# Per-head norms of a three-block kernel rewritten with compact roots, the third block's mixer outputs kept in SBUF, and two passes in the seven-product routine

## The chip, the cores and the metric

One core of a Trainium2 chip runs the whole program in one launch. The metric is device time in microseconds (us); lower is better. All data are float32. TensorE is called PE here, VectorE DVE, ScalarE ACT, GpSimd POOL, and SyncE (whose queue issues most transfers) SP.

## The reference, cut to what matters

Activations are 1024 positions by 1024 channels and pass through three blocks. The change touches the norms over single heads of 64 channels in blocks two and three, the end of the mixers of block three, and the gated and ungated MLPs of blocks three and one:

```python
def head_rmsnorm(o, gain):                                   # block 2: two mixers, 4 heads each, then * silu(gate)
    o = o * lax.rsqrt(jnp.mean(o * o, axis=-1, keepdims=True) + NORM_EPS_2)
...
    mean = jnp.mean(y, axis=-1, keepdims=True)               # block 3, rwkv: 8 heads
    var = jnp.mean(jnp.square(y - mean), axis=-1, keepdims=True)
    y = ((y - mean) * lax.rsqrt(var + LNX_EPS)).reshape(B, T, RWKV_DIM) * lnx_w + lnx_b
    y = y + bonus.reshape(B, T, RWKV_DIM)
    return y * g
...
    q = heads(rmsnorm(q.reshape(B, T, FOX_HEADS, HEAD_DIM), q_norm_w).reshape(B, T, FOX_DIM))   # block 3, fox
    k = heads(rmsnorm(k.reshape(B, T, FOX_HEADS, HEAD_DIM), k_norm_w).reshape(B, T, FOX_DIM))
...
    o = rmsnorm(o, o_norm_w).reshape(B, T, FOX_DIM)
    return o * jax.nn.sigmoid(og)
...
        x = x + jnp.concatenate([y_rwkv, y_fox], axis=-1) @ w_out[l].astype(jnp.float32)
        h = rmsnorm(x, norm_ffn_w[l])
        x = x + conv_glu_ffn(...)
```

## The kernel before

Activations lie transposed: 128 channels (two heads) on the partitions, 1024 positions along the free axis; such a 128x1024 tile is 512 KB. The program is a sequence of stages. Each `Stage` allocates its SBUF, PSUM and semaphores; when one that has semaphores ends, all engines meet at a barrier (L40), so nothing of the next stage starts before the slowest queue of this one is done, its stores included. Inside a stage each engine runs its own list and waits on semaphores.

`head_norm` (four calls: `hgn` in block two, `fqk`, `lnx` and `fon` in block three) takes one tile at a time from a scratch tensor in HBM: SP loads x, a gate and, in `lnx`, a bonus into one of three slots (L681 to L685; a slot is loaded again when its store has landed); ACT squares it (L721); PE multiplies with a 128x128 matrix of ones over each head, so that every row of the result holds its head's sum (L691); DVE makes the variance (L749); ACT takes the logarithm and the exponential (L93, L94); DVE makes a Newton step of three operations (L99 to L101) and the product with gain and root (L759); POOL multiplies with the gates and issues the store (L784 to L792). In `lnx`, PE and DVE first subtract the mean (L744).

`rwkv_and_fox` (stage `mix`) runs the two mixers of block three interleaved from one job list. Its outputs leave for HBM from POOL (wkv in 16 pieces, fox in 4); `lnx` and `fon` read them back and store to `y3`. `folded_project` then computes `w_out` (stage `p`) with Strassen-like seven products for each pair of output tiles: before the first product it loads its eight input tiles (`feed`, L497), and DVE makes sums of input tiles (L244 to L250). The residual X stays in SBUF for the whole of blocks one to three (`stream_x`), and is added in `scaled_sum` (`res3a`).

`Folded.products` is that routine of seven products, each accumulated over kp pairs of input tiles. In `mlp`, hidden tiles are made in groups ("up" jobs) and each group is followed by four "down" jobs; the first of these four calls `products` with `await_last`, which waits (`u_sums`) for DVE's sums of the last pair of hidden tiles (L448). kp is 4 in block one's MLP; in block three's (`mlp3`) it is 3 in three groups and 2 in the last.

## Time and profile before

| what | value |
|---|---|
| median of 3 runs | 5811.05 us (5807.86 to 5812.35) |
| the profiled execution | 5812.52 us, its span 5810.9 us |
| PE busy | 4890.9 us, 84% |
| DVE, ACT, POOL busy | 2521.5, 1119.2, 898.6 us |
| mean granted PE clock | 0.921 of full |

The span runs from the first to the last instruction; the profiled execution lasted 1.6 us longer than its span. Busy time of PE is modelled from a pipelined engine, so PE busy is not PE at its peak.

### The profile page before, as it was taken

How to read it: one execution, taken by the hardware profiler on the slowest of the kernel's cores; microseconds unless marked ns; L12 is line 12 of the kernel's file. 1: busy time of each engine (PE TensorE's matmuls, PEld its weight loads, DVE VectorE, ACT ScalarE, POOL GpSimd, SP SyncE). 2: the span in 40 equal slices, each digit the busy share in tenths (PEclk: the TensorE clock that was granted, in tenths of full speed). 3: DMA queues.
4: the chain of work that ended last, by engine and by line, in shares of the span. 5: the costliest groups of instructions: out<-in, count | busy, mean ns of one | idle time of the engine just before them, and what ended most of it. 6: DMA issues, size and time to landing. Idle time of an engine off the chain costs nothing. (4 is left out here: it accounts for less than half of the span.)

```text
span 5810.9 us, 44089 instructions
## 1 busy us (share of the span) xinstructions
PE 4890.9 (84%) x16320; PEld 2512.2 (43%) x16320; DVE 2521.5 (43%) x3261; ACT 1119.2 (19%) x1602; POOL 898.6 (15%) x674
## 2 busy tenths in 40 slices
PE   8988677899997988889858597857999728999995
PEld 3434343344443434335523243326888613444442
DVE  4305552634554212225334414554443344755755
ACT  1003231100001003333220101243344321110101
POOL 0014401222221110012011010000000031222220
PEclk9999898999998999889979798978999869999997
DMA  2121202111111221111131013332221121111111
GB/s 99 58 102 34 76 37 91 69 44 44 44 44 62 87 86 39 37 65 63 61 138 43 33 73 115 141 111 65 53 53 48 50 103 66 38 42 43 40 44 69
DMA packets 194463, 378.61 MB, mean 65 GB/s; under 512 B 102919, under 2 KB 104471, under 8 KB 193368
## 3 DMA queue, kind: packets, MB, share of 16 engines
q1 hardware_dynamic: 173320, 315.10, 16.0%
q0 software_dynamic: 12880, 46.14, 2.2%
q10 hardware_dynamic: 8064, 14.68, 0.7%
q8 instruction: 128, 2.10, 0.1%
q14 instruction: 71, 0.58, 0.0%
HBM read 270.84 MB, written 105.02 MB: 65 GB/s over the span
## 5 line engine op out<-in xcount | busy, mean ns | idle before, releaser
L157 PE MATMUL mlp_bank<-mlp_u,mlp_s 128*128 128x512 f32 x864 | 380.9, 597 | 0.0
L889 PE MATMUL first_acc<-first_h,first_w 128*128 128x512 f32 x768 | 332.9, 594 | 0.0
L157 PE MATMUL mlp_bank<-mlp_u,mlp_w 128*128 128x512 f32 x648 | 293.1, 604 | 38.8 <-DVEq L448 38.8
L157 PE MATMUL p_bank<-p_t,p_s 128*128 128x512 f32 x720 | 313.9, 592 | 0.0
L144 POOL TENSOR_TENSOR mlp_s<-mlp_w 128x512 f32<-128x512 f32 (+2 forms) x70 | 90.2, 1288 | 1330.2 <-DMA mlp_w<-in_w_up 749.0
L157 PE MATMUL mlp_bank<-stream_x,mlp_s 128*128 128x512 f32 x608 | 273.3, 592 | 0.0
L157 PE MATMUL mlp_bank<-mlp_x,mlp_s 128*128 128x512 f32 x608 | 273.3, 592 | 0.0
L157 PE MATMUL mlp_bank<-stream_x,mlp_w 128*128 128x512 f32 x608 | 267.1, 592 | 0.0
L157 PEld LDWEIGHTS mlp_bank<-mlp_u,mlp_s 128*128 128x128 f32 x864 | 166.0, 192 | 210.8 <-issue 208.6
L2598 PE MATMUL rwin_half<-in_h,rwin_w 128*128 128x512 f32 x512 | 237.5, 624 | 10.8 <-ACT rwin_half_out L2647 10.8
L215 ACT ACTIVATE mlp_p<-mlp_bank 128x512 f32<-128x512 f32 x70 | 41.4, 591 | 989.6 <-PE mlp_bank L157 989.6
L889 PEld LDWEIGHTS first_acc<-first_h,first_w 128*128 128x128 f32 x768 | 144.9, 190 | 186.4 <-issue 186.4
L157 PEld LDWEIGHTS p_bank<-p_t,p_s 128*128 128x128 f32 x720 | 136.8, 190 | 172.2 <-issue 169.6
L157 PEld LDWEIGHTS mlp_bank<-mlp_u,mlp_w 128*128 128x128 f32 x648 | 124.8, 193 | 197.4 <-issue 155.3
L225 DVE TENSOR_TENSOR mlp_sum_u<-mlp_bank,mlp_p 128x512 f32<-128x512 f32 x70 | 48.4, 692 | 349.9 <-PE mlp_bank L157 348.5
L1622 PE MATMUL stick_tile<-stream_x,stick_fw 128*128 128x512 f32 x384 | 185.4, 628 | 0.0
L157 PEld LDWEIGHTS mlp_bank<-mlp_x,mlp_s 128*128 128x128 f32 x608 | 115.5, 190 | 145.4 <-issue 141.6
L157 PEld LDWEIGHTS mlp_bank<-stream_x,mlp_s 128*128 128x128 f32 x608 | 115.5, 190 | 145.4 <-issue 142.8
L157 PEld LDWEIGHTS mlp_bank<-stream_x,mlp_w 128*128 128x128 f32 x608 | 115.5, 190 | 145.4 <-issue 145.2
L2039 PE MATMUL lin_tile<-stream_x,lin_w 128*128 128x512 f32 x384 | 176.4, 608 | 0.0
L2598 PEld LDWEIGHTS rwin_half<-in_h,rwin_w 128*128 128x128 f32 x512 | 101.8, 200 | 147.8 <-issue 133.7
L144 POOL TENSOR_TENSOR p_s<-p_w 128x512 f32<-128x512 f32 x30 | 39.8, 1327 | 803.0 <-DMA p_w<-in_w_in 519.6
(621 smaller groups left out, 8460.8 us busy)
## 6 DMA issues: line engine op xcount, KB each, us to landing
mlp_w<-in_w_up SPq DMA_DIRECT2D x76, 512.0 KB, 4.1
proj<-p_ev SPq DMA_DIRECT2D x38, 512.0 KB, 2.7
p_w<-in_w_in SPq DMA_DIRECT2D x36, 512.0 KB, 5.7
mlp_w<-in_w_down SPq DMA_DIRECT2D x32, 512.0 KB, 4.6
first_w<-in_w_in SPq DMA_DIRECT2D x24, 512.0 KB, 3.2
p_w<-in_w_out SPq DMA_DIRECT2D x24, 512.0 KB, 5.7
merge_g<-proj SPq DMA_DIRECT2D x8, 1536.0 KB, 8.1
mlp_w<-in_w_down SPq DMA_DIRECT2D x24, 384.0 KB, 3.5
```

The lines of the kernel that those rows point to most:

```text
L144: nc.gpsimd.tensor_tensor(s1, a21, a22, ALU.add).then_inc(self.sums_ready, 1)
L157: mm = nc.tensor.matmul(self.bank[product - 1][:, :], lhs[:, p, :], rhs(name, p), start=p == 0, stop=p == kp - 1)
L215: nc.scalar.activation(self.p1[:, :], self.bank[0][:, :], ACT.Copy).then_inc(self.copied, 1)
L225: ch.step(nc.vector.tensor_tensor(self.u[:, :], p6, self.p1[:, :], ALU.add))
L889: mm = nc.tensor.matmul(acc[m % 2][:, cs], W[m % 2][:, k * P:(k + 1) * P], H[:, k, cs], start=k == 0, stop=k == KD - 1)
L1622: mm = nc.tensor.matmul(tile_acc[:, :], fw[t % 2][:, k * P:(k + 1) * P], act_in[:, k, e * HT:(e + 1) * HT], start=k == 0, stop=k == KD - 1)
L2039: mm = nc.tensor.matmul(tile_acc[h][:, :], W[t % 2][:, k * P:(k + 1) * P], act_in[:, k, h * HT:(h + 1) * HT], start=k == 0, stop=k == KD - 1)
L2598: mm = nc.tensor.matmul(half_acc[h][:, :], W[t % 2][:, k * P:(k + 1) * P], act_in[:, k, h * HT:(h + 1) * HT], start=k == 0, stop=k == KD - 1)
```

## The change

`head_norm` is replaced by `compact_norm`. It holds all tiles of a call in SBUF, in groups of four tiles (eight heads). PE sums the squares of a group with a 128x8 matrix (`pick`) into one 8x1024 result, one row for each head. Variance, logarithm, exponential and Newton step run once for each group on 8 partitions, after one load of an ACT table set. PE spreads each root over its 64 channels by a product with an 8x128 matrix (`back`), into a ring of two PSUM tiles that DVE reads as operand. POOL applies gates ahead of the root instead of behind it; stores are issued by SP. In the kind "layer" the bonus and beta are multiplied with the gate on DVE and added at the end. `lnx` and `fon` become one call, `lfn`, that reads the mixer outputs from a tensor Y in SBUF, and `p32` multiplies this Y directly. X gives up its place in SBUF during the mixers: `n21` stores it to HBM (`kept2`) and `p32` loads it back (`also`, L501 of the kernel before: issued by POOL behind the last sums). With `await_last`, `products` now makes all seven products over the first kp-1 pairs, waits, and then adds the last pair to all seven.

```diff
+        def all_seven(pairs, fresh, done):
+            if fresh:
...
+            await_product("B11")
+            mm = some(1, a11, "B11", pairs)
+            if done:
+                mm.then_inc(self.phases_done, 1)
...
+        if await_last is None:
+            all_seven(range(kp), True, True)
+            all_seven(range(kp - 1), True, False)
             await_last()
...
+            all_seven([kp - 1], False, True)
...
-def head_norm(nc, name, src, dsts, heads_ones, width, gain, eps, scale=1.0, gate=None, gate_kind=None,
...
+def compact_norm(nc, name, X, groups, width, heads, pick_in, back_in):
...
+        var, root, fix = ([r.sb(f"{n}{gi}", [8, T]) for gi in range(NG)] for n in ("var", "root", "fix"))
...
+        total = [r.ps(f"total{gi}", [8, T]) for gi in range(NG)]
+        ring = [r.ps(f"ring{s}", [P, T]) for s in range(2)]
...
+                sp.dma_start(pick[:, :], pick_in).then_inc(picks_in, 16)
+                sp.dma_start(back[:, :], back_in).then_inc(picks_in, 16)
...
+                            sp.dma_start(x_of(gi, j), g["src"][j]).then_inc(x_in[gi, j], 16)
...
+                            sp.dma_start(G[gi, j][:, :], g["gate"][j]).then_inc(g_in[gi, j], 16)
...
+                            sp.dma_start(A[gi, j][:, :], g["add"][j]).then_inc(a_in[gi, j], 16)
...
+                        if g.get("dst") is not None:
+                            sp.wait_ge(finished, n)
+                            for a, b, d in g["dst"](j):
+                                sp.dma_start(d, x_of(gi, j)[a:b, :]).then_inc(sent, 16)
...
+                def sums(n):
+                    gi, j = sq_order[n]
+                    pe.wait_ge(sq_ready, n + 1)
+                    for cs in (LEFT, RIGHT):
+                        mm = nc.tensor.matmul(total[gi][:, cs], pick[:, 8 * j:8 * j + 8], sq[n % 4][:, cs],
+                                              start=j == 0, stop=j == len(groups[gi]["tiles"]) - 1)
+                    mm.then_inc(sq_used, 1)
...
+                for gi, j in mean_order:
...
+                        pe.wait_ge(ring_free, no - 1)
+                    both(ring[no % 2], heads[:, :], x_of(gi, j)).then_inc(ring_done, 1)
+                pe.wait_ge(picks_in, 32)
+                for n in range(len(sq_order)):
+                    sums(n)
+                for gi, g in enumerate(groups):
+                    pe.wait_ge(rstd_ready, gi + 1)
+                    for j in range(len(g["tiles"])):
+                        no = ring_no["back", gi, j]
...
+                            pe.wait_ge(ring_free, no - 1)
+                        both(ring[no % 2], back[:, j * P:(j + 1) * P], root[gi]).then_inc(ring_done, 1)
...
+                def roots(gi):
+                    act.wait_ge(var_ready, gi + 1)
+                    inverse_root(nc, ach, root[gi], var[gi][:, :], exp_ready)
+                for n, (gi, j) in enumerate(sq_order):
...
+                    if groups[gi]["kind"] == "layer":
+                        act.wait_ge(centred, mean_order.index((gi, j)) + 1)
+                    if n >= 4:
+                        act.wait_ge(sq_used, n - 3)
+                    nc.scalar.activation(sq[n % 4][:, :], x_of(gi, j), ACT.Square).then_inc(sq_ready, 1)
+                    if n == ends[gi] and groups[gi]["kind"] in ("sigmoid", "silu"):
+                        for i in range(len(groups[gi]["tiles"])):
+                            act.wait_ge(g_in[gi, i], 16)
+                            nc.scalar.activation(SG[gi, i][:, :], G[gi, i][:, :], ACT.Sigmoid).then_inc(sig_ready, 1)
+                nc.scalar.preload_act_table_set("natural_log_exp_and_others")
+                for gi in range(NG):
+                    roots(gi)
+            @block.gpsimd
+            def _(pool):
...
+                for key in pool_order:
...
+                    x, kind = x_of(gi, j), groups[gi]["kind"]
+                    pool.wait_ge(sq_ready, sq_no[key] + 1)
+                    pool.wait_ge(g_in[key], 16)
...
+                    if kind in ("silu", "layer"):
+                        ch.step(nc.gpsimd.tensor_tensor(x, x, G[key][:, :], ALU.mult))
+                    if kind != "layer":
+                        pool.wait_ge(sig_ready, gate_order.index(key) + 1)
+                        ch.step(nc.gpsimd.tensor_tensor(x, x, SG[key][:, :], ALU.mult))
+                    pool.sem_inc(gated, 1)
...
+                for gi, j in mean_order:
+                    dve.wait_ge(ring_done, ring_no["mean", gi, j] + 1)
...
+                    nc.vector.scalar_tensor_tensor(x_of(gi, j), ring[ring_no["mean", gi, j] % 2][:, :], -1.0 / width,
+                                                   x_of(gi, j), ALU.mult, ALU.add).then_inc(centred, 1)
+                    dve.wait_ge(centred, mean_order.index((gi, j)) + 1)
+                    dve.sem_inc(ring_free, 1)
+                def variance(gi):
+                    dve.wait_ge(sq_used, ends[gi] + 1)
+                    nc.vector.tensor_scalar(var[gi][:, :], total[gi][:, :], 1.0 / width, groups[gi]["eps"], ALU.mult, ALU.add)\
+                      .then_inc(var_ready, 1)
+                variance(0)
...
+                for gi, g in enumerate(groups):
+                    dve.wait_ge(exp_ready, gi + 1)
+                    newton(nc, ch, root[gi][:, :], var[gi][:, :], fix[gi][:, :])
+                    dve.sem_inc(rstd_ready, 1)
+                    if gi + 1 < NG:
+                        variance(gi + 1)
+                    if g["kind"] == "layer":
+                        for j in range(len(g["tiles"])):
...
+                            ch.step(nc.vector.scalar_tensor_tensor(A[gi, j][:, :], A[gi, j][:, :], g["beta"][j], G[gi, j][:, :],
+                                                                   ALU.add, ALU.mult))
+                    for j in range(len(g["tiles"])):
+                        no, x = ring_no["back", gi, j], x_of(gi, j)
+                        dve.wait_ge(ring_done, no + 1)
...
+                        if g["kind"] != "plain":
+                            dve.wait_ge(gated, pool_no[gi, j] + 1)
+                        ch.step(nc.vector.scalar_tensor_tensor(x, x, scaled_gain[:, n:n + 1], ring[no % 2][:, :],
+                                                               ALU.mult, ALU.mult))
+                        dve.sem_inc(ring_free, 1)
+                        if g["kind"] == "layer":
+                            ch.step(nc.vector.tensor_tensor(x, x, A[gi, j][:, :], ALU.add))
+                        dve.sem_inc(finished, 1)
...
-def scaled_sum(nc, name, x, alpha, y, store=None):
+def scaled_sum(nc, name, x, alpha, y, dst=None, store=None):
...
-                        nc.scalar.activation(YO[c % 2][:, :, :], of(job)[:, :, 0:CK], ACT.Copy).then_inc(kept["y"], 1)
+                        nc.scalar.activation(Y[:, 0:NP, c * CK:(c + 1) * CK], of(job)[:, :, 0:CK], ACT.Copy).then_inc(kept["y"], 1)
...
-                        nc.vector.tensor_copy(Y[h // 2 % 2][e, i * P:w], O[e, 0:P]).then_inc(o_kept, 1)
+                        nc.vector.tensor_copy(Y[e, NP + h // 2, i * P:w], O[e, 0:P]).then_inc(o_kept, 1)
...
-                        pool.dma_start(wkv_out[c], YO[c % 2][:, :, :]).then_inc(y_sent[c % 2], 16)
-                        pool.dma_start(fox_out[j], Y[j % 2][:, :]).then_inc(fox_sent[j % 2], 16)
...
+    heads = np.arange(P)[:, None, None] // 64 + 2 * np.arange(4)[None, :, None] == np.arange(8)[None, None, :]
...
+    c["back"] = heads.transpose(2, 1, 0).reshape(8, 4 * P)
...
-            head_norm(nc, "hgn", lambda j: heads2[j * P:(j + 1) * P, :],
...
+            with Stage(nc, "hgnx") as q:
+                hx = q.sb("x", [P, 4, T])
+                compact_norm(nc, "hgn", [hx[:, j, :] for j in range(4)],
+                             [{"kind": "silu", "tiles": range(4), "src": [heads2[j * P:(j + 1) * P, :] for j in range(4)],
...
-                normalise(nc, "n21", M, X, ones, col["ln_g"], EPS2, beta=col["ln_b"])
+                normalise(nc, "n21", M, X, ones, col["ln_g"], EPS2, beta=col["ln_b"], store=tile_rows(kept2))
...
-            head_norm(nc, "fqk", lambda j: proj3[f0 + j * P:f0 + (j + 1) * P, :],
...
+            with Stage(nc, "fqkx") as q:
+                hx = q.sb("x", [P, 8, T])
...
+                def split_heads(to):
+                    return lambda j: [(h * HD, (h + 1) * HD, to[2 * j + h, 0:HD, :]) for h in range(2)]
+                compact_norm(nc, "fqk", [hx[:, j, :] for j in range(8)],
+                             [{"kind": "plain", "tiles": range(4 * i, 4 * i + 4), "scale": (HD ** -0.5, 1.0)[i], "eps": EPS,
+                               "src": [proj3[f0 + j * P:f0 + (j + 1) * P, :] for j in range(4 * i, 4 * i + 4)],
+                               "gain": columns(col[("fq", "fk")[i]]), "dst": split_heads((qa, ka)[i])} for i in range(2)],
...
-            head_norm(nc, "lnx", lambda j: wkv[j * P:(j + 1) * P, :], lambda j: [(0, P, y3[j * P:(j + 1) * P, :])],
...
-            head_norm(nc, "fon", lambda j: fox[j * P:(j + 1) * P, :], lambda j: [(0, P, y3[512 + j * P:512 + (j + 1) * P, :])],
...
+        with Stage(nc, "tail") as tail:
+            Y = tail.sb("y", [P, KD, T])
+            rwkv_and_fox(nc, rw, qa, ka, proj3[f0 + 1024:f0 + 1536, :], c["chunk_mask"], c["chunk_wide"], c["causal"], ident, Y)
+            compact_norm(nc, "lfn", [Y[:, j, :] for j in range(8)],
+                         [{"kind": "sigmoid", "tiles": range(4, 8), "eps": EPS, "gain": columns(col["fo"]),
+                           "gate": [proj3[f0 + 1536 + j * P:f0 + 1536 + (j + 1) * P, :] for j in range(4)]},
+                          {"kind": "layer", "tiles": range(4), "eps": 64e-5, "gain": columns(col["lnx_w"]),
+                           "beta": columns(col["lnx_b"]), "add": [rw["bonus"][j * P:(j + 1) * P, :] for j in range(4)],
+                           "gate": [rw["gate"][j * P:(j + 1) * P, :] for j in range(4)]}], HD, heads64, c["pick"], c["back"])
             with Stage(nc, "out3") as q:
-                Y, M = q.sb("y", [P, KD, T]), q.sb("m", [P, KD, T])
-                folded_project(nc, "p32", Y, a["w_out3"], KD, dst=M, feed=[tile_rows(y3)[n] for n in range(KD)])
-                scaled_sum(nc, "res3a", M, 1.0, X, store=tile_rows(kept3))
+                M, X = q.sb("m", [P, KD, T]), q.sb("x", [P, KD, T])
+                folded_project(nc, "p32", Y, a["w_out3"], KD, dst=M, also=(X[:, :, :], rows(kept2)))
+                scaled_sum(nc, "res3a", M, 1.0, X, dst=Y, store=tile_rows(kept3))
+            X = Y
```

## Rows read from the trace of the kernel before

**Rows 1.** Windows: hgn, fqk, mix, lnx, fon, p32's matmuls, res2 with n21.
```profile
core 0: us, PE busy (x) PEld busy (x) DVE busy (x) ACT busy (x) POOL busy (x), PEclk, DMA share, GB/s
2886.50:2952.60 66.10, 12.80 (x16) 4.44 (x16) 28.96 (x24) 32.19 (x28) 21.98 (x12) 0.55 0.25 95
3836.70:3924.60 87.90, 25.17 (x32) 8.33 (x32) 49.12 (x48) 45.66 (x40) 8.48 (x16) 0.62 0.33 96
3940.70:4604.30 663.60, 608.16 (x4832) 557.75 (x4832) 266.68 (x573) 256.84 (x521) 13.74 (x19) 0.97 0.20 48
...
4610.60:4694.70 84.10, 20.18 (x32) 7.67 (x32) 39.94 (x32) 22.83 (x20) 23.70 (x12) 0.60 0.25 100
4694.70:4755.40 60.70, 12.85 (x16) 4.38 (x16) 25.22 (x24) 32.19 (x28) 11.71 (x8) 0.58 0.28 104
...
4772.00:4871.30 99.30, 98.59 (x224) 43.30 (x224) 30.38 (x44) 2.39 (x4) 9.94 (x8) 0.98 0.07 23
...
3189.00:3261.50 72.50, 32.74 (x64) 13.69 (x64) 39.69 (x37) 13.13 (x12) 0.00 (x0) 0.74 0.00 0
```

**Rows 2.** Groups by tile and line: duration ns min/median/max, first and last start.
```profile
L99 DVE TENSOR_TENSOR fqk_fix<-fqk_rstd x8: 1212/1216/1224, 3849.6 to 3912.4; 128x1024 f32<-128x1024 f32 x8
...
L749 DVE TENSOR_SCALAR fqk_var<-fqk_total x8: 1215/1224/1225, 3844.9 to 3906.3; 128x1024 f32<-128x1024 f32 x8
...
L759 DVE SCALAR_TENSOR_TENSOR fqk_x<-fqk_x,fqk_gain,fqk_rstd x8: 1284/1284/1285, 3853.4 to 3916.2; 128x1024 f32<-128x1024 f32 x8
...
L786 POOL TENSOR_TENSOR hgn_x<-hgn_x,hgn_g x4: 2328/2336/2343, 2907.4 to 2943.1; 128x1024 f32<-128x1024 f32 x4
...
L2165 ACT ACT_TABLE_LOAD  x1: 1283/1283/1283, 2591.1 to 2591.1; - x1
```

**Rows 3.** Timeline of ACT in fqk: the first two squares.
```profile
3839.90 1.06 ACT L721 ACTIVATE fqk_sq<-fqk_x 128x1024 f32<-128x1024 f32 x1 [6.44 <-DMA fqk_x<-proj]
3841.17 1.06 ACT L721 ACTIVATE fqk_sq<-fqk_x 128x1024 f32<-128x1024 f32 x1 [0.22 <-DMA fqk_x<-proj]
```

**Rows 4.** DVE in lnx beside a busy POOL; DVE operation with a PSUM operand.
```profile
4679.73 3.25 DVE L101 SCALAR_TENSOR_TENSOR lnx_rstd<-lnx_fix,lnx_rstd 128x1024 f32<-128x1024 f32 x1
...
4678.69 3.20 POOL L786 TENSOR_TENSOR lnx_x<-lnx_x,lnx_g 128x1024 f32<-128x1024 f32 x1
...
L225 DVE TENSOR_TENSOR mlp_sum_u<-mlp_bank,mlp_p x70: 690/692/693, 1077.1 to 5743.7; 128x512 f32<-128x512 f32 x70
```

**Rows 5.** Timeline of PE in lnx: two tiles, then one tile.
```profile
4616.92 6.86 PE L691 MATMUL lnx_mean<-lnx_x,main_heads 128*128 128x512 f32 x8 [12.94 <-DMA lnx_a<-rw_bonus]
4623.62 1.88 PE L691 MATMUL lnx_total<-lnx_sq,main_heads 128*128 128x512 f32 x4
```

**Rows 6.** Timeline around res3a: a bare barrier, and one behind stores.
```profile
4872.34 9.17 DVE L2440 SCALAR_TENSOR_TENSOR stream_x<-out_m,stream_x 128x1024 f32<-128x1024 f32 x8 [1.00 <-PEq L40]
...
4886.09 2.00 ACT L364 ACTIVATE mlp3m_m<-stream_x 128x1024 f32<-128x1024 f32 x2 [35.44 <-PEq L40]
```

**Rows 7.** Timeline of p32's start.
```profile
4755.40 43.95 SPq L133 DMA_DIRECT2D p_w<-in_w_out  x6
...
4773.25 3.21 DVE L244 TENSOR_TENSOR p_t<-out_y 128x512 f32<-128x512 f32 x4 [25.01 <-DMA out_y<-y]
...
4760.44 1.26 POOL L144 TENSOR_TENSOR p_s<-p_w 128x512 f32<-128x512 f32 x1 [0.41 <-DMA p_w<-in_w_out]
...
4772.02 9.32 PE L157 MATMUL p_bank<-out_y,p_w 128*128 128x512 f32 x16 [39.63 <-DMA out_y<-y]
```

**Rows 8.** PE's waits in mlp3: their sum, the first, the last.
```profile
  PE mlp_bank L157: 38.8, 4
...
5063.92 3.78 PE L157 MATMUL mlp_bank<-mlp_u,mlp_w 128*128 128x512 f32 x4 [9.02 <-DVEq L448]
5067.49 8.30 PE L157 MATMUL mlp_bank<-mlp_u,mlp_s 128*128 128x512 f32 x16
...
5699.40 3.78 PE L157 MATMUL mlp_bank<-mlp_u,mlp_w 128*128 128x512 f32 x4 [11.77 <-DVEq L448]
```

More of the change, by code:

```diff
@@ L166, in await_bank @@
                 pe.wait_ge(self.banks_free, 4 * (n - 1) + count)
-        now, late = range(kp), []
-        if await_last is not None:
-            now, late = range(kp - 1), [kp - 1]
-        self.await_weights(pe, n)
-        if n:
-            pe.wait_ge(self.copied, n)
-        await_product("B11")
-        mm = some(1, a11, "B11", now)
-        if not late:
-            mm.then_inc(self.phases_done, 1)
-        await_bank(1)
-        await_product("B21")
-        mm = some(2, a12, "B21", now)
@@ L571, in normalise @@
             if store is not None:
-                assert add_to is not None
+                assert add_to is not None or beta is not None
                 @block.sync
@@ L675, in _ @@
             def _(sp):
-                for j in range(N):
-                    s = j % 3
-                    if j >= 3:
-                        sp.wait_ge(stored[s], 16 * len(dsts(0)) * (j // 3))
-                    sp.dma_start(X[s][:, :], src(j)).then_inc(loaded[s], 16)
-                    if gate is not None or times is not None:
-                        sp.dma_start(G[s][:, :], (gate or times)(j)).then_inc(loaded[s], 16)
-                    if add is not None:
-                        sp.dma_start(A[s][:, :], add(j)).then_inc(loaded[s], 16)
+                sp.dma_start(pick[:, :], pick_in).then_inc(picks_in, 16)
@@ L687, in _, with both @@
             @block.tensor
             def _(pe):
[L689 to L708 removed]
+                def both(out, lhs, x):
+                    for cs in (LEFT, RIGHT):
+                        mm = nc.tensor.matmul(out[:, cs], lhs, x[:, cs], start=True, stop=True)
+                    return mm
@@ L737, in _ @@
                 ch = Chain(dve, own)
-                for j in range(N):
-                    ins = nc.vector.tensor_scalar(scaled_gain[:, j:j + 1], gain[j], scales[j], None, ALU.mult)
-                ch.step(ins)
-                def take_mean(j):
-                    dve.wait_ge(mean_ready, j + 1)
-                    nc.vector.scalar_tensor_tensor(X[j % 3][:, :], mean[j % 2][:, :], -1.0 / width, X[j % 3][:, :],
-                                                   ALU.mult, ALU.add).then_inc(centred, 1)
@@ L2448, in _ @@
                         sp.wait_ge(own, k + 1)
-                        sp.dma_start(store[k], y[:, k, :]).then_inc(stored, 16)
+                        sp.dma_start(store[k], dst[:, k, :]).then_inc(stored, 16)
                     sp.wait_ge(stored, 16 * KD)
@@ L2805, in mix_jobs, with rwkv_and_fox @@
     return jobs
[L2808 removed]
+def rwkv_and_fox(nc, src, q, k, v, masks_in, wide_in, causal_in, ident, Y):
     NP = RH // 2
@@ L2842, in rwkv_and_fox @@
         PT = r.sb("pt", [P, KD, P])
-        Y = [r.sb(f"y{s}", [P, T]) for s in range(2)]
         st = r.sb("st", [P, 2, 4])
@@ L3489, in build @@
-            head_norm(nc, "lnx", lambda j: wkv[j * P:(j + 1) * P, :], lambda j: [(0, P, y3[j * P:(j + 1) * P, :])],
-                      heads64, HD, columns(col["lnx_w"]), 64e-5, centre=True, beta=columns(col["lnx_b"]),
-                      add=lambda j: rw["bonus"][j * P:(j + 1) * P, :], times=lambda j: rw["gate"][j * P:(j + 1) * P, :])
-            head_norm(nc, "fon", lambda j: fox[j * P:(j + 1) * P, :], lambda j: [(0, P, y3[512 + j * P:512 + (j + 1) * P, :])],
-                      heads64, HD, columns(col["fo"]), EPS, gate=lambda j: proj3[f0 + 1536 + j * P:f0 + 1536 + (j + 1) * P, :],
-                      gate_kind="sigmoid")
+            with Stage(nc, "fqkx") as q:
[6 more added lines that the diff above has]
+                               "gain": columns(col[("fq", "fk")[i]]), "dst": split_heads((qa, ka)[i])} for i in range(2)],
+                             HD, heads64, c["pick"], c["back"])
```

261 lines of the change are left out of this document (108 added, 153 removed).

## The prediction

> **What bounds the kernel now.** I read the busy times first: PE is busy 84% of the span, but that is a mean over stages, so the windows by stage come next [rows 1]: each row gives the length of a stage and how long each engine was busy in it. In mix and in p32 PE works nearly all the time (608.2 of 663.6 us, 98.6 of 99.3). In the four calls of the head norm no engine does: in fqk PE is busy 25.2 of 87.9 us, DVE 49.1, ACT 45.7, and the DMA engines a third. These stages are chains: load, square, sum, root, Newton, product, store, with three slots between the loads and the stores. Together hgn, fqk, lnx and fon take 66.1 + 87.9 + 84.1 + 60.7 = 298.8 us. Since every stage ends in a barrier, a microsecond won in a norm is a microsecond of the end, and only what is won inside a stage behind PE counts nothing. The last views are the start of p32, where PE waits for input tiles that were just stored [rows 7], and PE's waits in mlp3 [rows 8].
>
> **Prices.** A 512 KB load lands 3.2 us after its issue and then one each 1.27 us [rows 3]; the stage and its first issue began at 3836.7 [rows 1]. ACT takes 1.06 for 1024 columns [rows 3], a table load 1.28 [rows 2]. DVE takes 1.22 for an operation of 1024 columns and 1.28 for the product with gain and root; POOL 2.34 [rows 2]. The change works on 8 partitions instead of 128 in variance, root and Newton step. No row prices that shape; an operation can hardly be dearer than on 128, and it walks the same 1024 columns, so I take 1.06 and 1.22, with nothing as the lower bound. PE needs 3.44 us for a tile of two halves at 1.2 GHz (8 records in 6.86 us) and 1.72 at 2.4 GHz [rows 5], the two levels of its clock; PE had idled 12.9 us before the stretch at the lower one. The products with `pick` and `back` stream the same 512 columns, so I price them as L691. A bare barrier costs 1.0; from DVE's last operation (4872.34 + 9.17 = 4881.5) behind a store to the next stage's first work it is 4.6 [rows 6].
>
> When DVE and POOL both work on SBUF, one DVE operation took 3.25 instead of 1.22 and one of POOL 3.20 instead of 2.34; with an operand in PSUM DVE's time stayed at 0.69 in all 70 cases [rows 4]. The Trainium skill (SBUF — State Buffer, section "SBUF: two separate sides") says that a DVE operation with two SBUF inputs and a GpSimd operation exclude each other and the loser blocks for the whole operation. That speaks against this change, which puts the gates of POOL beside the Newton step; by that rule alone a Newton operation could wait 2.3 us, about what the row shows, and the trace agrees.
>
> **hgn.** Times from the stage's start. Two small constants are issued first (0.8), then x and gate in turn: x lands at 4.0, 6.6, 9.1, 11.7. The last square ends at 12.7, PE's sums at 15.6, the variance at 16.8. ACT goes on after the squares: table 1.3, four sigmoids 4.3, table 1.3, root 2.1, so 21.8. That is later than the variance; ACT sets this step. The Newton step costs 3.7 alone. POOL has eight products, seven of them behind the first sigmoid (15.1): 7 x 2.4 = 17, so until 32 to 35, beside the Newton step, which may therefore take up to 3 x 3.25 = 9.8. The root is ready between 25.6 and 31.6; I take 29. PE has been idle since 15.6, so two of four tiles run at the lower clock: 10.3. DVE's last product is at 40.9, the store and barrier add 4.6: 46, against 66.1. Gain 20 (42 to 51, so 15 to 24).
>
> **n21.** The store of X to `kept2` is new. Its first seven tiles hide behind DVE's remaining products; the last adds 4.6 - 1.0. Loss 3.7 (3 to 5), on a stage chain of 72.5 us [rows 1].
>
> **fqk.** Eight tiles land from 4.0 to 12.9. PE's sums, in order and two of them at the lower clock, set the step: first group at 15.5, second at 22.3. Group one: variance 16.8, ACT free of its squares and its table load at 17.9, root 20.1, Newton 23.9. PE then spreads four tiles (until 31) and DVE multiplies behind it until 32.4. DVE does the Newton step of group two only then: 36.2. PE has idled for 5; four tiles take 7 at the upper clock or 10.3 with two at the lower: last product at 46, plus 4.6: 51, against 87.9. There is no POOL work in it. Gain 37 (33 to 40).
>
> **mix, lnx, fon.** DVE's last copy in mix ends at 4604.3, p32 starts at 4755.4: 151.1 us for the drain of the last stores, lnx and fon. In their place: barrier 1.0, lfn, barrier 1.0, no store at all. In lfn no input is awaited: Y is there. PE makes the four means (to 11), the sums of eight tiles follow to 24.5; ACT squares and makes the sigmoids beside it. Root of the fox group at 22, Newton beside POOL's last gates until 28 (26 free of POOL), variance of group two, PE's four tiles and DVE's products until 38. Then Newton 3.7, four times bonus plus beta times gate 5.0, four times product and sum 10.2: 57. PE's tiles of this group run under the 5.0 and cost nothing; without that cover, with PE at the lower clock, they would add 3. The twelve loads (12 x 1.27 + 4 = 19 us) land before DVE wants them. lfn 57 (52 to 64), in all 59 against 151.1. Gain 92 (85 to 97). Inside mix 20 stores go and their waits with them; they were covered by PE's 608 busy us, so I count nothing (a loss of 1 to a gain of 2).
>
> **p32.** It started PE at 4772.0, 16.6 us into the stage, though POOL had weights at 5.0. With Y in SBUF PE starts at 5.0. What is late next are DVE's sums of input tiles, 3.2 us for each of four kinds; they start at 0.3 and the first is done at 3.5, under PE's first two products of 9.3 us [rows 7]. Gain 11.7 (10 to 13). The load of X (eight times 1.27, about 10 us) is issued behind POOL's last sums, when PE is about half through its 99 us; it is hidden. Nobody queues behind it.
>
> **mlp3.** PE waits 38.8 us in four places for DVE's last sums: three times 9.0 and once 11.8 [rows 8]. The end of the wait is DVE's and stays. Moved ahead of it are three products over kp-1 pairs, of 0.86 us each: 3 x 2 x 0.86 = 5.15 in three groups, 3 x 0.86 = 2.6 in the last: 18.0. After the first wait 20 records took 11.9 us, where the upper clock takes 8.6 + 0.15; with a shorter idle some of this 3 us comes back: 3 in all (0 to 9). Against it: all seven results now finish within 6.0 us, and the next job waits for banks that DVE frees. DVE's four quarters are about 9 us of work in an accumulating job, but the next job needs them over its own first 5 us; I count up to 3. Gain 21 (16 to 27). mlp1 has no such wait to take from, and its PE never stops there: 0 (a loss of up to 2).
>
> **Sum.** 20 - 3.7 + 37 + 92 + 11.7 + 21 = 178.0 us. The profiled execution took 5812.5 us, 1.7 outside its span; the median of the runs is 5811.05, 1.5 lower. The change touches nothing outside the span: 5811 - 178 = 5633 us. All low ends give 151, all high ends 200.
>
> **Rivals.** (1) The chains stay long: POOL and DVE block each other through both gated norms and PE stays at 1.2 GHz in every product with `back`. For it: the norms ran at 0.55 to 0.62 of the clock [rows 1] and the 3.25 us row; against it: fqk has no POOL work, and lfn's PE hides. It costs 5 in hgn, 4 in fqk, 9 in lfn and 10 in mlp3's banks and p32 together, with 10 more for waits I don't see: 5640 to 5675, say 5665. The Trainium skill's rule (SBUF — State Buffer, section "SBUF: two separate sides") leads to this case, since a blocked DVE operation and a blocked GpSimd operation then hold each other up for as long as both have work. (2) More comes back than I count, because 8 partitions are cheaper, the clock stays up, or mix runs quicker without its stores; at 3% of mix's 663.6 us that is 20: 5600. (3) The seven-product change does not do what it says: PE waits for a bank where it waited for a sum. Its 21 us are lost: 5654. Against it: DVE frees the banks of the job before while PE makes 6.9 us of early products. (4) Slower: the outputs of mix written straight into Y hold up mix. There are 16 copies by ACT and 64 by DVE on its chain; the gain of 178 is gone when each costs 178 / 80 = 2.2 us more, that is when mix takes 27% longer. At 3 us each it is 5873. Against it: the same engines make the same number of copies of the same size, only the address differs.
>
> **Chances and range.** Forecast 0.74, rival 1 0.10, rival 2 0.07, rival 3 0.07, rival 4 0.02. The range 5604 to 5666 takes in all low and high ends and rival 3, and leaves out the far parts of 1 and 2. Two tenths of a per cent, 12 us, is what a measurement of this kernel can tell from no change: faster 0.97, within 0.01, slower 0.02.
>
> **What the profile would show.** lfn between 52 and 64 us long with no store; hgn about 46, fqk about 51; one table load before the roots of each call; PE's first product in p32 5 us after its first weight issue; PE's four waits in mlp3 at 3.9, 3.9, 3.9 and 9.2. The prediction is wrong if Newton steps on 8 partitions take much less or more than 3.7, if PE's products with 8 rows or 8 columns cost other than 0.43 a record, if a new wait stands in front of PE in mlp3, or if mix is not 663 us.

## The result and the profile after

The changed kernel took 5645.93 us (median of 4 runs, 5641.68 to 5659.12) against 5811.6 us for the kernel before on the same chip: a ratio of 0.972, with an interval of 0.9703 to 0.9737. The forecast was 5633 us with a range of 5604 to 5666; the gain is 165.7 us where 178 were forecast. The profiled execution took 5648.0 us, its span 5646.3.

First the windows by stage, as in [rows 1]: hgn, fqk, mix, lfn (which has the place of lnx and fon), p32.

```profile
core 0: us, PE busy (x) PEld busy (x) DVE busy (x) ACT busy (x) POOL busy (x), PEclk, DMA share, GB/s
2890.00:2940.09 50.09, 22.86 (x32) 6.52 (x32) 15.44 (x12) 12.80 (x12) 20.96 (x8) 0.60 0.32 127
...
3819.52:3879.70 60.18, 40.96 (x64) 12.30 (x64) 20.52 (x24) 13.95 (x13) 0.00 (x0) 0.65 0.46 140
3894.47:4554.77 660.30, 606.02 (x4832) 555.54 (x4832) 266.80 (x573) 255.63 (x520) 0.00 (x0) 0.98 0.18 43
4555.90:4619.39 63.49, 48.98 (x80) 15.77 (x80) 40.21 (x36) 18.81 (x18) 20.88 (x8) 0.71 0.26 100
4620.29:4726.30 106.01, 99.24 (x224) 43.56 (x224) 35.57 (x43) 2.39 (x4) 24.19 (x17) 0.94 0.21 80
```

The stages add up to the difference of the spans, 164.6 us:

| stretch | before, us | after, us | gain | forecast |
|---|---|---|---|---|
| start to hgn | 2886.5 | 2890.0 | -3.5 | 0 |
| hgn | 66.1 | 50.1 | 16.0 | 20 |
| hgn's end to fqk (with n21) | 884.1 | 879.4 | 4.6 | -3.7 |
| fqk | 87.9 | 60.2 | 27.7 | 37 |
| forget | 16.1 | 14.8 | 1.4 | 0 |
| mix | 663.6 | 660.3 | 3.3 | 0 |
| end of mix to p32 | 151.1 | 65.5 | 85.6 | 92 |
| p32 to the end | 1055.5 | 1026.0 | 29.5 | 32.7 |

Where the gain of a norm comes from shows in ACT's groups of fqk, before and after (busy time, mean of one, then the idle time ahead):

```profile
L93 ACT ACT_TABLE_LOAD x8 | 10.3, 1283 | 0.1
L94 ACT ACT_TABLE_LOAD x8 | 10.3, 1283 | 0.1
L721 ACT ACTIVATE fqk_sq<-fqk_x 128x1024 f32<-128x1024 f32 x8 | 8.4, 1052 | 29.8 <-DMA fqk_x<-proj 29.8
...
L771 ACT ACT_TABLE_LOAD x1 | 1.3, 1283 | 0.0
L766 ACT ACTIVATE fqk_sq<-fqkx_x 128x1024 f32<-128x1024 f32 x8 | 8.4, 1056 | 10.2 <-DMA fqkx_x<-proj 10.2
```

Sixteen table loads became one and sixteen root operations four, but ACT's waits for x also fell from 29.8 to 10.2 us, since no load waits for a slot any more. No run takes the fewer roots and the missing slots apart.

What fell short is hgn, fqk and lfn by 19.7 us together, and the last stretch by 3.2. In hgn, DVE's timeline shows the Newton step, PE's the product with `back`, and DVE's again the products behind it.

```profile
2912.10 2.28 DVE L99 TENSOR_TENSOR hgn_fix<-hgn_root 8x1024 f32<-8x1024 f32 x1 [5.43 <-ACT hgn_root L94]
2914.41 3.24 DVE L100 SCALAR_TENSOR_TENSOR hgn_fix<-hgn_fix,hgn_var 8x1024 f32<-8x1024 f32 x1
2917.69 3.24 DVE L101 SCALAR_TENSOR_TENSOR hgn_root<-hgn_fix,hgn_root 8x1024 f32<-8x1024 f32 x1
...
2921.05 14.02 PE L723 MATMUL hgn_ring<-hgn_root,hgn_back 8*128 8x512 f32 x16 [15.71 <-DVEq L818]
...
2928.28 1.28 DVE L834 SCALAR_TENSOR_TENSOR hgnx_x<-hgnx_x,hgn_gain,hgn_ring 128x1024 f32<-128x1024 f32 x1 [2.13 <-PE hgn_ring L723]
```

The Newton step takes 8.8 us; I had allowed up to 9.8 and counted a part of it. The four tiles of the spread take 14.02 us, which is 16 records at 1.2 GHz, to the last one: I had written 10.3. Behind the first tile DVE waits 2.13 us for PE in each. The granted clock of this stretch is 0.50; in lfn the sums with `pick` ran at 1.00:

```profile
core 0: us, PE busy (x) PEld busy (x) DVE busy (x) ACT busy (x) POOL busy (x), PEclk, DMA share, GB/s
2921.05:2935.07 14.02, 14.02 (x16) 5.14 (x16) 3.84 (x3) 0.00 (x0) 4.43 (x2) 0.50 0.27 107
4562.98:4576.88 13.90, 13.90 (x33) 2.80 (x32) 4.62 (x4) 9.66 (x10) 12.30 (x6) 1.00 0.79 316
```

The spreads in fqk are the more telling, since to the first of them PE comes from products at 2.4 GHz (its timeline):

```profile
3834.73 5.31 PE L730 MATMUL fqk_total<-fqk_sq,fqk_pick 128*8 128x512 f32 x12
3842.23 11.62 PE L723 MATMUL fqk_ring<-fqk_root,fqk_back 8*128 8x512 f32 x16 [2.19 <-DVEq L818]
3859.25 14.02 PE L723 MATMUL fqk_ring<-fqk_root,fqk_back 8*128 8x512 f32 x16 [5.40 <-DVEq L818]
```

At 0.43 us a record at the upper clock and 0.876 at the lower (14.02 / 16), 11.62 us are about five records at the upper clock and eleven at the lower: PE was busy all the time and its clock fell.

In mlp3 PE's waits went as forecast, three of 3.88 us and one of 9.16 (their sum in the view of the waits, then the first in PE's timeline), against [rows 8].

```profile
PE mlp_bank L157 <- DVEq L454: 20.8, 4, 9.2
```

```profile
4920.17 3.52 PE L157 MATMUL mlp_bank<-mlp_u,mlp_w 128*128 128x512 f32 x4 [3.88 <-DVEq L454]
4923.53 3.60 PE L157 MATMUL mlp_bank<-mlp_u,mlp_s 128*128 128x512 f32 x8
```

### The profile page after: what moved, and what is told of

Its sections match the earlier page's. It is cut to its first block and busy times, and to the rows that moved or that the text cites. A ratio compares the mean times of both kernels' runs of the same rounds, so it can differ in the third digit from the quotient of the medians.

```text
span 5646.3 us, 44066 instructions
## 1 busy us (share of the span) xinstructions
PE 4932.6 (87%) x16400; PEld 2520.4 (45%) x16400; DVE 2466.3 (44%) x3205; ACT 1026.9 (18%) x1525; POOL 862.3 (15%) x615
## 5 line engine op out<-in xcount | busy, mean ns | idle before, releaser
L157 PE MATMUL mlp_bank<-mlp_u,mlp_w 128*128 128x512 f32 x648 | 293.3, 603 | 20.8 <-DVEq L454 20.8
L157 PE MATMUL mlp_bank<-tail_y,mlp_s 128*128 128x512 f32 x352 | 158.2, 592 | 0.0
L157 PE MATMUL mlp_bank<-tail_y,mlp_w 128*128 128x512 f32 x352 | 154.7, 592 | 0.0
L221 ACT ACTIVATE p_p<-p_bank 128x512 f32<-128x512 f32 x30 | 17.9, 597 | 748.6 <-PE p_bank L157 748.6
L157 PE MATMUL mlp_bank<-mlp_x,mlp_w 128*128 128x512 f32 x304 | 136.7, 592 | 0.0
```

Source lines behind the costliest of these rows:

```text
L157: mm = nc.tensor.matmul(self.bank[product - 1][:, :], lhs[:, p, :], rhs(name, p), start=p == 0, stop=p == kp - 1)
L221: nc.scalar.activation(self.p1[:, :], self.bank[0][:, :], ACT.Copy).then_inc(self.copied, 1)
```

## The experiments

Nine edited kernels and the changed kernel once more. Lengths in us from the first DMA issue of a stage to that of the next; lfn has its barriers with it, and fqk is taken to the third issue of forget, so it is 0.7 longer here than above.

| run | time | ratio | hgn | to fqk | fqk | to lfn | lfn | p32 to the end |
|---|---|---|---|---|---|---|---|---|
| changed | 5645.9 | 0.9720 | 50.1 | 879.4 | 60.9 | 675.5 | 64.4 | 1026.0 |
| changed, again | 5645.9 | 0.9717 | 49.7 | 873.5 | 63.3 | 678.7 | 64.4 | 1026.7 |
| old products | 5668.2 | 0.9761 | 50.9 | 879.0 | 61.2 | 677.2 | 64.4 | 1043.8 |
| 128 rows | 5626.6 | 0.9689 | 46.0 | 876.8 | 52.5 | 675.7 | 59.1 | 1025.5 |
| PE kept busy | 5636.3 | 0.9704 | 47.5 | 877.3 | 60.3 | 675.6 | 62.2 | 1024.7 |
| gate on DVE | 5641.5 | 0.9719 | 45.1 | 878.1 | 63.2 | 678.1 | 62.3 | 1026.3 |
| combined | 5627.4 | 0.9685 | 43.9 | 882.1 | 50.7 | 677.8 | 60.1 | 1024.9 |
| round trip | 5693.9 | 0.9801 | 50.0 | 872.6 | 63.5 | 678.6 | 12.9 + 86.2 | 1036.7 |
| 32 rows | 5648.1, one run | | 50.1 | 876.3 | 61.0 | 677.5 | 64.1 | 1027.0 |
| 64 rows | 5641.5, one run | | 50.1 | 879.9 | 55.6 | 675.8 | 64.1 | 1027.1 |
| balanced | 5621.6 | 0.9673 | 43.5 | 871.1 | 50.3 | 677.7 | 58.0 | 1026.6 |

The intervals of the ratios are 0.0013 to 0.0017 to either side. The stretch from hgn to fqk is the same code in all eleven and runs from 871.1 to 882.1; hgn began anywhere from 2886.6 to 2893.8. So these two rows of the table of gains (-3.5 and 4.6) can't be read to the microsecond. Where its code is the changed kernel's, hgn repeats within 1.2 (49.7 to 50.9), fqk within 2.6 (60.9 to 63.5, the gate on DVE among them, which alters nothing in fqk) and lfn within 0.1.

**The control.** 

> The changed kernel itself, as the measure for the runs beside it. Stage lengths should repeat within 1 us (hgn 50, fqk 60, lfn 64), the beginning of hgn anywhere between 2886 and 2894 as in the runs so far, and the time 5640 to 5650 us.

 Time, hgn and lfn are as expected; fqk is 2.4 us longer than in the first profile, so it repeats less well than I wrote: its sums took 16.69 us where they had taken 15.32, and the first spread 13.03 where it had taken 11.62.

**The old products.**

```diff
-            all_seven(range(kp - 1), True, False)
             await_last()
-            all_seven([kp - 1], False, True)
+            some(1, a11, "B11", late).then_inc(self.phases_done, 1)
+            some(2, a12, "B21", late).then_inc(self.phases_done, 1)
+            some(5, s1, "T1", late).then_inc(self.phases_done, 1)
+            some(7, s3, "T3", late).then_inc(self.phases_done, 1)
...
+        some(6, s2, "T2", range(kp)).then_inc(self.phases_done, 1)
```

> The changed kernel with the products of mlp3 in the old order (T1, T3 and the last pair before T2, B22 and T4). Theory (the wait of PE shrinks by the moved products, 18.0 us, and some 3 us of clock come back): PE waits 38.8 us again in mlp3, three times 9.0 and once 11.8, the stage is 18 to 21 us longer and the kernel takes 5664 to 5667 us. Rival (the moved products cost as much in waits for banks in the next job): under 5 us, 5646 to 5651. A side question: in the changed kernel hgn begins 3.5 us later than before; if the new order does that in mlp1, hgn begins near 2886.5 here, otherwise near 2890.

 5668.2 us, 22.3 more and 1.2 above my range; the profiled spans differ by 20.6. The view of waits has 38.8 us again. The last stretch is 17.8 us longer, but it holds two stages that moved apart: p32 with res3a is 2.0 shorter here (119.6 against 121.6, its weights land earlier), and mlp3, from ACT's first operation in it to the end, is 19.9 longer (924.3 against 904.4; the kernel before has 924.8). The waits account for 18.0. In the other nine profiles with the new order mlp3 takes 904.2 once and 906.0 to 906.8 eight times, so of the 3 us of clock that I added some 2 were there in two profiles of ten and none in the rest. The rival of the banks falls. hgn began at 2890.3, but with the new order it began anywhere from 2886.6 to 2893.8, so this one value settles nothing about the side question.

```profile
PE mlp_bank L157 <- DVEq L448: 38.8, 4, 11.7
```

**128 rows.**

```diff
-        pick, back, picks_in = r.sb("pick", [P, 32]), r.sb("back", [8, 4 * P]), r.sem("picks_in")
+        pick, back, picks_in = r.sb("pick", [P, 32]), r.sb("back", [P, 4 * P]), r.sem("picks_in")
...
+                for gi in range(NG):
+                    nc.gpsimd.memset(root[gi][:, :], 0.0).then_inc(zeroed, 1)
```

Here root is [P, T], and `back` is filled up with zero rows and loaded behind the inputs. 

> The root tile and the matrix `back` have 128 rows, 120 of them zero, so the product that spreads the root is 128x128 by 128x512 as in the kernel before. Theory (a product of 8 rows leaves PE at 1.2 GHz, one of 128 rows lets it rise): four tiles take 10.4 to 10.6 us instead of 14.0 where PE had idled, and about 7 in the first group of fqk instead of 11.6; hgn 3.4 us shorter, fqk 3 to 8, lfn 3 to 5, in all 10 to 15: 5631 to 5636 us. Rival A (the clock is low only because PE had idled, and four tiles are too short for it to rise): 14.0 us stay, 5646. Rival B (zero rows do no work, so 120 more of them change nothing): 14.0 and 11.6 stay, 5646.

 5626.55 us, 19.4 less, more than I expected; 17.8 of it lies in the three norms. PE's timeline, the spreads of hgn and of fqk:

```profile
2922.26 9.70 PE L724 MATMUL hgn_ring<-hgn_root,hgn_back 128*128 128x512 f32 x16 [15.79 <-DVEq L823]
...
3836.35 7.11 PE L724 MATMUL fqk_ring<-fqk_root,fqk_back 128*128 128x512 f32 x16 [2.28 <-DVEq L823]
3848.85 8.93 PE L724 MATMUL fqk_ring<-fqk_root,fqk_back 128*128 128x512 f32 x16 [5.39 <-DVEq L823]
```

The idle time ahead (15.79, 2.28, 5.39) is as in the changed kernel; and 14.02, 11.62 and 14.02 become 9.70, 7.11 and 8.93. The edit also loads `back` later and clears the roots on POOL, but so do the runs with 32 and 64 rows below, where a spread from idle stays at 14 us; what is left is the rows. Both rivals fall: the 120 added rows hold zeros, and the clock rises with them. Two windows inside the spread of hgn show it:

```profile
2922.26:2926.00 3.74, 3.74 (x5) 1.67 (x6) 0.00 (x0) 0.00 (x0) 3.66 (x2) 0.50 0.02 4
2927.00:2931.96 4.96, 4.96 (x11) 1.65 (x9) 2.89 (x3) 0.00 (x0) 0.00 (x0) 0.95 0.49 198
```

**PE kept busy.**

```diff
+                for _ in range({"hgn": 8, "fqk": 1, "lfn": 3}[name]):
+                    both(ring[0], heads[:, :], sq[(len(sq_order) - 1) % 4])
                 for gi, g in enumerate(groups):
                     pe.wait_ge(rstd_ready, gi + 1)
```

> PE makes unused products of 128 rows while it waits for the first root: 8 tiles' worth in hgn, 1 in fqk, 3 in lfn, so that it comes to the products with `back` at 2.4 GHz. Theory (the 8-row product itself pulls the clock down, as in the first group of fqk, where PE came to it 2.2 us after products at the upper clock and 16 records took 11.6 us): a first group takes 11 to 12 us instead of 14.0, so hgn and lfn are 2 to 3 us shorter each, fqk the same: 5640 to 5642 us. Rival (the idle time ahead is what sets the clock): a first group takes 7 us, hgn, fqk and lfn are 7, 4 and 6 us shorter: 5629 us. The second groups of fqk and lfn stay at 14.0 by both.

 hgn and lfn are 2.6 and 2.2 us shorter, as by the theory, and fqk 0.6, less than it moves by itself. The profiled span is 5.0 lower (5641.3 against 5646.3), as the stages have it; the median is 9.7 lower and below my range. The profiled execution was the slowest of its four (5643.0 against 5634.7 to 5637.8), and what the other 4 are isn't shown. PE's timeline in hgn, and two windows inside the spread:

```profile
2909.55 14.00 PE L723 MATMUL hgn_ring<-hgn_sq,main_heads 128*128 128x512 f32 x32
2925.34 10.90 PE L723 MATMUL hgn_ring<-hgn_root,hgn_back 8*128 8x512 f32 x16 [1.80 <-DVEq L822]
```

```profile
2925.34:2927.50 2.16, 2.16 (x5) 1.03 (x6) 0.14 (x1) 0.00 (x0) 2.09 (x1) 1.00 0.00 0
2928.00:2936.20 8.20, 8.20 (x11) 2.76 (x9) 3.20 (x3) 0.00 (x0) 1.86 (x1) 0.53 0.45 181
```

PE came in at 1.00 and was at 0.53 in the second window, with no idle time between. In fqk PE had no idle time ahead of the first spread either, only products of 128 rows at 1.00. The clock fell all the same:

```profile
3840.53 1.98 PE L723 MATMUL fqk_ring<-fqk_sq,main_heads 128*128 128x512 f32 x4
3842.45 9.84 PE L723 MATMUL fqk_ring<-fqk_root,fqk_back 8*128 8x512 f32 x16
...
3842.45:3846.00 3.55, 3.55 (x10) 1.54 (x10) 2.28 (x2) 2.11 (x2) 0.00 (x0) 1.00 0.00 0
3847.50:3852.20 4.70, 4.70 (x6) 1.33 (x4) 1.28 (x1) 0.00 (x0) 0.00 (x0) 0.50 0.83 236
```

A PE that comes in at the upper clock is not kept there by this product.

**32 and 64 rows.** The edit is that with 128 rows, with another number. 

> As the run with 128 rows, but root and `back` have 32 rows. If what pulls the clock down scales with the rows, 32 of them should be nearer to 8 than to 128: four tiles take 13 to 14 us from idle, and the first group of fqk falls to the lower clock later or not at all. If any width over 8 will do, they take 9 to 10 us, as 128 rows do.

 

> Root and `back` with 64 rows, between the 32 at which nothing changed and the 128 at which four tiles took 7.1 to 9.7 us. If the clock goes by the share of rows, something between: a group from idle in 10 to 13.5 us, and the first group of fqk falls late. If it has an edge between 32 and 128, a group takes either 14.0 or 9 to 10.

 PE's timeline with 32 rows, hgn then fqk, and with 64 rows in fqk:

```profile
2921.52 13.99 PE L724 MATMUL hgn_ring<-hgn_root,hgn_back 32*128 32x512 f32 x16 [15.78 <-DVEq L823]
...
3839.53 11.77 PE L724 MATMUL fqk_ring<-fqk_root,fqk_back 32*128 32x512 f32 x16 [2.43 <-DVEq L823]
```

```profile
3839.19 7.10 PE L724 MATMUL fqk_ring<-fqk_root,fqk_back 64*128 64x512 f32 x16 [1.78 <-DVEq L823]
3851.69 14.02 PE L724 MATMUL fqk_ring<-fqk_root,fqk_back 64*128 64x512 f32 x16 [5.39 <-DVEq L823]
```

32 rows are as 8. With 64 rows PE stayed at the upper clock in the one group to which it came at it (7.10) and never rose in the four to which it came from idle (14.02 here, 13.99 in hgn, 13.99 and 14.02 in lfn). My second guess had the 14.0 but not the 7.10, the first neither. Both kernels ran once; their times are not compared, only the groups.

**The gate on DVE.**

```diff
-                    if kind != "layer":
-                        pool.wait_ge(sig_ready, gate_order.index(key) + 1)
-                        ch.step(nc.gpsimd.tensor_tensor(x, x, SG[key][:, :], ALU.mult))
+                        if (gi, j) in SG:
+                            dve.wait_ge(sig_ready, gate_order.index((gi, j)) + 1)
+                            ch.step(nc.vector.tensor_tensor(x, x, SG[gi, j][:, :], ALU.mult))
```

> POOL keeps the products x by gate; the products by the sigmoid (four in hgn, four in lfn) are made by DVE just ahead of its product with gain and root, where it waits 2.1 us for PE in each tile. Theory (DVE and POOL block each other on SBUF): the Newton step of hgn takes 3.7 us instead of 8.8, that of lfn 3.7 to 6 instead of 8.4, and the moved products hide under PE: hgn 5 us shorter, lfn 2 to 5, kernel 5636 to 5639 us. Rival A (the Newton step is slow because of its 8 partitions or because DVE starts late on a root that ACT just wrote): 8.8 and 8.4 stay and the kernel takes 5646. Rival B (the moved products don't hide, DVE becomes the bound of the tiles): 8 x 1.25 = 10 us more, which takes back what the Newton step gives: 5646 to 5649.

 hgn is 5.0 us shorter and lfn 2.1, as expected; the median is only 4.4 lower, above my range. In its profile fqk, which the edit doesn't touch, is 2.3 longer and mlp3 2.1 (906.5 against 904.4), both within what they move by. Both rivals fall in hgn: the Newton step is quick, and the moved products hide. DVE's timeline in hgn:

```profile
2909.02 1.21 DVE L99 TENSOR_TENSOR hgn_fix<-hgn_root 8x1024 f32<-8x1024 f32 x1 [5.43 <-ACT hgn_root L94]
2910.26 1.21 DVE L100 SCALAR_TENSOR_TENSOR hgn_fix<-hgn_fix,hgn_var 8x1024 f32<-8x1024 f32 x1
2911.51 1.21 DVE L101 SCALAR_TENSOR_TENSOR hgn_root<-hgn_fix,hgn_root 8x1024 f32<-8x1024 f32 x1
```

The same three operations took 2.28, 3.24 and 3.24 us beside POOL. On 8 partitions they cost what they cost on 128 [rows 2], 1.21 us. The Trainium skill (SBUF — State Buffer, section "SBUF: two separate sides") says that a DVE operation with two SBUF inputs and a GpSimd operation that reads SBUF shut each other out; the trace agrees, with 2.0 us more for a DVE operation. In lfn POOL's four products x by gate are still beside the Newton step, and one operation of it took 3.25.

**The round trip put back.** A stage of its own stores the eight tiles of Y to `y3` behind mix; lfn gets `src` and `dst` in `y3`:

```diff
+                           "src": [tile_rows(y3)[j] for j in range(4, 8)], "dst": lambda j: [(0, P, tile_rows(y3)[4 + j])],
...
-                folded_project(nc, "p32", Y, a["w_out3"], KD, dst=M, also=(X[:, :, :], rows(kept2)))
+                folded_project(nc, "p32", Y, a["w_out3"], KD, dst=M, feed=[tile_rows(y3)[n] for n in range(KD)],
+                        also=(X[:, :, :], rows(kept2)))
```

> The changed kernel with the round trip put back: an own stage stores Y to `y3` behind mix, lfn loads its eight tiles from there and stores them again, and p32 feeds from `y3`. Theory (of the 86 us gained between mix and p32 some 35 are the round trip, the rest the new design): the storing stage takes 12 to 15 us, of which the kernel before hid all but about 5 in mix; lfn takes 85 to 92 us instead of 64, since PE waits for the last of 20 loads (4 + 17 x 1.27 = 25.6 us) before it squares; PE starts in p32 some 10 us later: 5690 to 5700 us. Rival (loads hide in lfn as they do in hgn and fqk, and nearly all of the gain is design): lfn at most 70, 5670 to 5680.

 5693.9 us, 48.0 more. The storing stage takes 12.9, lfn 86.2 instead of 64.4, and PE starts in p32 at 4671.40, 16.6 us into the stage, as it did before [rows 7], instead of 4.9 to 6.8. PE's timeline:

```profile
4584.35 6.63 PE L723 MATMUL lfn_ring<-tail_y,main_heads 128*128 128x512 f32 x8 [30.06 <-DMA tail_y<-y]
...
4671.40 8.98 PE L157 MATMUL p_bank<-tail_y,p_w 128*128 128x512 f32 x16 [23.21 <-DMA tail_y<-y]
```

The three lengths and the total are as the theory had them, but its "some 35" for the round trip was too much: 27.0. The gain of 85.6 us between mix and p32 splits so: 21.8 (86.2 - 64.4) are loads and stores of the norm; 5.2 are the wait for mix's last stores (6.3 us from DVE's last copy to lnx before, 1.1 to lfn after); the remaining 58.6 are what is left for the design: one call instead of two, one root for eight heads, no slots. No run splits them.

**Combined, then balanced.** Three edits in one (128 rows, the sigmoid's products on DVE, and the second Newton step ahead of the third product of group one):

```diff
                         dve.sem_inc(finished, 1)
+                        if j == 1 and gi + 1 < NG:
+                            step(gi + 1)
```

> Three edits together: `back` and root with 128 rows, the products by the sigmoid on DVE, and DVE's Newton step of the second group ahead of the third product of the first group instead of behind the fourth (in fqk and lfn), so that PE goes from group to group without the 5.4 us of idle time. Theory (what is left of the norms is a chain PE to DVE at the lower clock plus the DVE queue): hgn 50.1 to 41 us, fqk 60.2 to 46 (8.4 by the rows, 6 by the order), lfn 64.4 to 51 to 54, in all 33 to 36 us, 5610 to 5613 us. Rival (the three gains overlap, because DVE becomes the bound of each tile once PE is at 2.4 GHz: 1.23 + 1.28 + waits = 3.1 us where there is a gate): the order of the Newton step is worth nothing in lfn and the gate 2 us less in each: 20 to 24 us, 5622 to 5626.

 5627.4 us: no better than 128 rows alone. The rival's account holds, though its 5622 to 5626 was still too low. With PE at 2.4 GHz a tile with a gate costs DVE 2.96 us (from one product with gain and root to the next), and PE stands idle; hgn gains 2.1 us more, fqk 1.8, lfn loses 1.0. In fqk the early Newton step leaves PE 3.61 us idle, because both slots of the ring are full while DVE is at the root.

The last kernel leaves lfn's sigmoid products on POOL and moves the four operations bonus plus beta times gate (L825) into DVE's idle time:

```diff
+                prepare(mean_order[0:1])
                 variance(0)
+                prepare(mean_order[1:2])
...
+                step(0)
+                prepare(mean_order[2:])
```

> `back` and root with 128 rows; the sigmoid's products on DVE in hgn only; the second Newton step ahead of the third product of the first group; in lfn the four operations bonus plus beta times gate where DVE waits (one ahead of the first variance, one behind it, two behind the second). Theory (with PE at 2.4 GHz DVE's queue is the bound of lfn, so what counts is how much of it lies in DVE's idle time): hgn 44, fqk 51, lfn 53 us against 44, 51 and 60 in the combined run, so 20 us below the changed kernel in all, 5620 to 5624 us. Rival (the operations moved ahead block POOL's gates on SBUF and the gates become late instead): lfn 57 to 60, 5625 to 5629 us.

 5621.6 us, a ratio of 0.9673 (0.966 to 0.9686), the lowest median of all; the interval of the run with 128 rows (0.9672 to 0.9705) overlaps it. But lfn is 58.0, as by the rival, and not 53: POOL's gates took 2.73 to 3.84 us beside the moved operations and ended at 4567.8, 32.1 into the stage (29.4 in the changed kernel), so that two of the three Newton operations still took 3.25. POOL's timeline, the last two of its products by the sigmoid:

```profile
4547.69 2.73 POOL L793 TENSOR_TENSOR tail_y<-tail_y,lfn_sg 128x1024 f32<-128x1024 f32 x1 [0.57 <-ACT lfn_sq L768]
4550.69 3.84 POOL L793 TENSOR_TENSOR tail_y<-tail_y,lfn_sg 128x1024 f32<-128x1024 f32 x1 [0.27 <-POOL tail_y L793]
```

Compared with 128 rows alone the norms give 5.8 us in sum (46.0 + 52.5 + 59.1 against 43.5 + 50.3 + 58.0), close to the 6.3 between the profiled spans and the 4.9 between the medians.

## Why the prediction was right, and where its terms were off

- **The main mechanism was right.** The norms were chains; fewer root steps, no slots, one stage fewer and no round trip gave 129.3 of the 165.7 us, where 149 were forecast for hgn, fqk and the stretch from mix to p32. Of the stretch from mix to p32 the round trip is 27.0; fewer roots and the missing slots were not taken apart.
- **The total owes something to luck.** By spans the gain is 164.6 of 178.0. The norms and the last stretch fell 22.9 short. The stretches for which I counted nothing, or a loss, gave 9.5 more than forecast: 8.3 between hgn and fqk, 3.3 in mix, 1.4 in forget, less 3.5 ahead of hgn. Most of that is no larger than what unchanged code moves by.
- **The spread was mis-sized.** The step "two of four tiles run at the lower clock: 10.3" was taken from [rows 5], a product of 128 rows. The product of the change has 8. It took 14.02 in four groups and 11.62 in one. With 128 rows hgn, fqk and lfn come out 4.1, 8.4 and 5.3 us shorter, which is the size of the 4.0, 9.3 and 6.4 that they fell short (fqk by itself moves by 2.6). I had written that "the products with `pick` and `back` stream the same 512 columns, so I price them as L691"; that was right for `pick`, whose operand has 128 rows, and wrong for `back`. The Trainium skill (TensorE: Matmul & The Clock Gate, section "Part 1: The HAM clock gate") says that the throttled state is the default and activity releases it, and makes no condition of the shape. By that, a spread of 8 rows without a gap would have come up to 2.4 GHz, as the one of 128 rows did (9.70 us). The trace differs (14.02 us, granted clock 0.50), and the measurement decides.
- **Rival 1 was half true.** PE ran at 1.2 GHz through four of the five groups of products with `back` and through most of the fifth, and DVE and POOL blocked each other in both gated norms. Its 18 us for this (5, 4 and 9) are near the 19.7 that the norms fell short, but by stage it was 4.0, 9.3 and 6.4: fqk, which I held up against it, lost most. The runs give 17.8 for the clock and 7.1 for the gates, some of which my sum already held. Of its 10 for mlp3's banks and p32, 3.2 are missing in that stretch, and the 10 of waits are not there. Its terms add up to 38, so my number for it should have been 5671 and not 5665; rival 2's 20 us likewise give 5613 and not 5600.
- **Newton beside POOL.** It took 8.8 us in hgn and 8.4 in lfn, near the upper bound of 9.8; in hgn it ended 30.9 us into the stage (29 forecast, 31.6 the upper end).
- **Cost on 8 partitions.** 1.21 us, the upper bound, was the right end.
- **n21.** The store costs 2.5 us (3.43 from DVE's last operation to n31's first, 0.88 before), 3.7 forecast.
- **p32.** PE started 6.8 us into the stage, 5.0 forecast: the weights land between 4.9 and 6.8 us, from run to run. DVE's third and fourth kind of sums took 5.70 and 6.54 us beside POOL's instead of 3.21. PE's first sixteen records took 10.15 us instead of 9.32. PE's start gained 9.8 for 11.7, and p32 with res3a is 9.1 shorter (130.7 to 121.6).
- **mlp3.** The 18.0 us were exact in the waits (38.8 to 20.8). The stage itself is 20.4 shorter in the first profile (924.8 to 904.4), but 18.0 to 18.8 in eight of the ten profiles with this order, so the 3 us of clock were mostly not there.
- **Mix.** 3.3 us shorter, where I counted nothing and at most 2; no run here takes this apart, and unchanged stretches move by more from run to run. forget is 1.4 shorter, without its table load: the call before it left ACT with the set it wants. I had left that out.
- **Open.** Why a product of few rows keeps the clock down is not shown, only that it goes with the rows: idle time ahead was the same (15.7, 2.2 and 5.4 us), products with 8 output columns ran at 1.00, and rows of zeros counted as rows. Which part of the gain in hgn, fqk and lfn comes from fewer roots and which from the missing slots is not shown. How the gain before fqk is split between the change and chance is open too.

## What to carry to other kernels

A step that is made small by a reduction to a few partitions is not cheaper on DVE or ACT, and it can hold TensorE at 1.2 GHz where it is an operand of a product: price such a product at the lower clock throughout, or fill it up with zero rows to the full 128, which lengthened no stage here. When that wait goes, look for who queues next; here it was DVE: in the lengths of the norms 128 rows were worth 17.8 us and the gate on DVE 7.1, and both with a third edit 20.7. Take a stage's gain from stage lengths in the trace when the edits are worth 5 us, and check that no other stage shares the stretch: unchanged stretches of this kernel move by up to 11 us (871.1 to 882.1).
